# Latent attention of a two-block layer: tile-pipelined scores, rotary queries turned for two heads at once, the gated product in halves

## The reference

```python
q = (_rmsnorm(q_lat, q_lat_w) @ w_uq).reshape(B, L, 8, 128 + 64)
kv = (_rmsnorm(kv_lat, kv_lat_w) @ w_ukv).reshape(B, L, 8, 128 + 128)
q_nope, q_pe = q[..., :128], q[..., 128:]
k_nope, v = kv[..., :128], kv[..., 128:]
q_nope, k_nope = _rmsnorm(q_nope, qn_w), _rmsnorm(k_nope, kn_w)
q_pe = _rope(_rmsnorm(q_pe, qpe_w), cos, sin)
k_pe = _rope(_rmsnorm(k_pe, kpe_w), cos, sin)
s = q_nope @ k_nope.T + q_pe @ k_pe.T            # per head, 512 queries x 528 keys
p = softmax(s * 192 ** -0.5)
y_mla = (p @ v) * silu(g_mla)                    # g_mla: 1024 columns of the input projection
h_res = h_res + concat([y_mla, y_na]) @ w_out
```

## Time and profile before

| | |
|---|---|
| median of 3 runs (lowest to highest) | 1404.66 us (1404.48 to 1405.96) |
| profiled execution: its time, its span | 1407.8 us, 1406.1 us |
| PE busy, weight loads busy | 95%, 76% of the span |
| DVE, ACT, POOL busy | 51%, 36%, 43% |
| scores of head 0 to scores of head 7 (first tiles) | 792.56 to 984.33 us |
| last head and output projection, to the first product of the neighbourhood attention | 984.33 to 1055.88 us |

### The profile page before, as it was taken

The page is one execution under the profiler, slowest core; times in us unless marked ns, Lnnn a source line. Parts: engine busy times, 40 slices in busy tenths (PEclk is TensorE's granted clock), DMA queues, the critical chain, the costliest instruction groups (busy, mean ns, idle before and its releaser), DMA issues.

```text
span 1406.1 us, 20334 instructions
## 1 busy us (share of the span) xinstructions
PE 1335.3 (95%) x6958; PEld 1066.1 (76%) x6958; DVE 716.9 (51%) x1347; ACT 501.9 (36%) x1042; POOL 605.7 (43%) x366
## 2 busy tenths in 40 slices
PE   7999999998999999999985899999899999999997
PEld 6877777875888888888874677787778888888765
DVE  4237766644565565621142577777434544444441
ACT  3233333313333333310022566666202444444420
POOL 5423323363444445555530543544154655555511
PEclk9999999999999999999997999999989999999999
DMA  6322222232333333332331111111033322222112
GB/s 181 96 64 77 70 75 76 69 96 60 92 98 94 94 100 90 94 116 83 98 90 31 45 30 46 30 44 43 17 104 101 84 69 67 67 70 71 60 33 73
DMA packets 196561, 105.40 MB, mean 75 GB/s; under 512 B 18982, under 2 KB 194444, under 8 KB 196508
## 3 DMA queue, kind: packets, MB, share of 16 engines
q1 hardware_dynamic: 196060, 104.00, 26.0%
q0 software_dynamic: 432, 0.69, 0.2%
q10 hardware_dynamic: 16, 0.00, 0.0%
HBM read 102.57 MB, written 2.10 MB: 74 GB/s over the span
## 4 chain that ended last, share of the span: by engine, by line
PE 82%; issue 5%; DVE 4%; POOL 4%; ACT 3%; DMA 1%; SPq 0%; DVEq 0%; POOLq 0%; ACTq 0%
PE ps L348 20%; PE ps L349 19%; PE ps L350 19%; PE ps L370 9%; PE ps L1232 1%; PE ps L1262 1%; PE ps L1243 1%; POOL w_low L335 1%; PE ps L1265 1%; POOL y_low L656 1%; DMA x_tok<-in_x_dram 1%; PE ps L893 1%; PE ps L1286 1%; POOL sq L637 1%; PE ps L915 1%
## 5 line engine op out<-in xcount | busy, mean ns | idle before, releaser
L335 POOL TENSOR_TENSOR w_low<-w_raw,w_high 128x1024 fp32r<-128x1024 f32 x183 | 447.7, 2448 | 539.1 <-DVE w_high L330 539.0
L348 PE MATMUL ps<-h_high,w_high 128*128 128x512 f32 x864 | 353.5, 409 | 11.8 <-DVE h_low L471 8.4
L349 PE MATMUL ps<-h_low,w_high 128*128 128x512 f32 x864 | 343.8, 398 | 0.0
L350 PE MATMUL ps<-h_high,w_low 128*128 128x512 f32 x864 | 342.6, 397 | 0.0
L348 PEld LDWEIGHTS ps<-h_high,w_high 128*128 128x128 f32 x864 | 163.8, 190 | 62.3 <-issue 20.6
L330 DVE CAST w_high<-w_raw 128x1024 fp32r<-128x1024 f32 x183 | 137.3, 752 | 139.1 <-PE ps L350 75.1
L350 PEld LDWEIGHTS ps<-h_high,w_low 128*128 128x128 f32 x864 | 163.9, 190 | 37.7
L349 PEld LDWEIGHTS ps<-h_low,w_high 128*128 128x128 f32 x864 | 164.0, 190 | 35.2 <-issue 1.7
L2047 DVE SCALAR_TENSOR_TENSOR z<-ps,cv,z 128x511 f32<-128x511 f32 x44 | 33.0, 750 | 97.8 <-ACT z L1516 97.8
L1516 ACT ACTIVATE z<-ps,cv 128x512 f32<-128x512 f32 x44 | 34.3, 779 | 121.9 <-PE ps L350 121.7
L350 PE MATMUL ps<-m_high,w_low 128*128 128x512 f32 x176 | 69.4, 395 | 0.0
(11 more groups left out here) (327 smaller groups left out, 2405.7 us busy)
## 6 DMA issues: line engine op xcount, KB each, us to landing
w_raw<-in_w_in_dram SPq DMA_DIRECT2D x150, 256.0 KB, 3.2
w_raw<-in_w_up_dram SPq DMA_DIRECT2D x88, 256.0 KB, 3.1
w_raw<-in_w_out_dram SPq DMA_DIRECT2D x44, 256.0 KB, 3.0
w_raw<-in_w_down_dram SPq DMA_DIRECT2D x32, 256.0 KB, 3.0
w_raw<-in_w_down_dram SPq DMA_DIRECT2D x16, 192.0 KB, 2.7
rel<-in_rel_bias_dram SPq DMA_DIRECT2D x8, 384.0 KB, 3.2
x_tok<-in_x_dram SPq DMA_DIRECT2D x4, 512.0 KB, 5.8
w_raw<-in_w_ob_dram SPq DMA_DIRECT2D x8, 256.0 KB, 2.8
```

What stands on the lines that cost most here:

```text
L335: pool.tensor_tensor(w_low[:, n % RING, :], w_raw[:, n % RAW, :], w_high[:, n % RING, :].bitcast(F32), ALU.subtract).then_inc(low_made, 1)
L348: pe.matmul(acc, wh, mh, start=first and k == 0, stop=False)
L349: pe.matmul(acc, wh, ml, start=False, stop=False)
L350: done = pe.matmul(acc, wl, mh, start=False, stop=last and k == tiles - 1)
```

## The change

1. Rotary queries for two heads at once: the strip of an even head now has in its extra 64 columns the rotary columns of the next, odd head (`twice`), so that the 128 output rows hold both heads. `m_project(0)`, `m_sums(0)`, `m_rotate`, the square, the root and `m_rope` are then done for even heads alone. `q_pe` is a tile of its own. The low part of the rotary query is made per head on VectorE (`m_pe_low`), where GpSimd did it before.
2. `head` becomes `head_then_even` and `head_then_odd`, by the parity of the next head. In both, the scores of tile t + 1 stand ahead of the turning of tile t, and the turning of tile 3 moves into the next head. Scores wait for `s_exp`; the meta corner moves from bank 1 to the first 128 columns of bank 6, and so its transpose waits, in tiles 0 and 2, for the gated product (`s_y`) that reads them.
3. The scale is in the gains of the queries (`mq_gain`), the maximum is negated by the reduction, and ScalarE's small negating operation goes away. The main part of the probabilities is scaled ahead of the meta part.
4. The gate has two buffers (`mg`), and the gated product goes into a tile of its own (`gy`) in two halves.
5. `last_head`: more of the early output projection stands behind turnings, and strip `N_OM` + 3 is made early too. GpSimd makes strips `N_OM` + 6 and + 7 ahead of the bias table.

```diff
+                q_pe = sb("q_pe", [P, S], F32, a)[:]
+                a.enter_context(nc.sbuf_tensor("y_low_", [P, 7, S], F32))
+                gy = sb("gy", [P, S], F32, a)[:]
...
-                        ("twice", 704, 64, q[:, :, bass.ds(i * 96 + g * 192 + 128, 64)])]
+                        ("twice", 704, 64, q[:, :, bass.ds(i * 96 + g * 192 + (320 if g % 2 == 0 else 128), 64)])]
...
+            def m_pe_low(i, c):
+
+                dve.wait_ge(s["x_high"], i * 6 + (3 * c + 2))
+                own, other = (slice(h * 64, h * 64 + 64) for h in (c % 2, 1 - c % 2))
+                dve.tensor_tensor(qpe_parts[other, c % 2, :], q_pe[own, :], qpe_parts[own, c % 2, :].bitcast(F32),
+                                  ALU.subtract).then_inc(s["xp_low"], 1)
...
             pool.wait_ge(s["tables_in"], 64)
+            for n in range(N_OM + 6, N_OM + 8):
+                make_low(pool, n)
             bias_table(0, 0)
-            for n in range(N_OM + 6, N_NA + 5):
+            for n in range(N_OM + 8, N_NA + 5):
...
                 if not first:
-                    pe.wait_ge(s["s_meta"], i * 16 + (8 * c + 2 * t))
+                    pe.wait_ge(s["s_exp"], i * 8 + (4 * c + t))
...
-                pe.transpose(ps[0:80, 1, 3 * P:4 * P], me_meta[:, t % 2, :], ident[:])\
+                if t == 2 or c and t == 0:
+                    pe.wait_ge(s["s_y"], i * 4 + (2 * c + t // 2))
+                pe.wait_ge(s["s_probs"], i * 16 + (8 * c + 2 * t + 2))
+                pe.transpose(ps[0:80, 6, 0:P], me_meta[:, t % 2, :], ident[:])\
                     .then_inc(s["s_turned"], 1)
...
+            def head_then_even(i, c):
+
+                m_turn(i, c - 1, 3)
+                m_project(i, c + 1, 0)
+                m_project(i, c + 1, 1)
+                m_weigh(i, c - 1, 1)
+                m_sums(i, c + 1, 0)
+                m_scores(i, c, 1)
+                m_turn(i, c, 0)
+                m_gate(i, c + 1, 0)
+                m_sums(i, c + 1, 1)
+                m_rotate(i, c + 1)
+                m_scores(i, c, 2)
+                m_turn(i, c, 1)
+                m_project(i, c + 1, 3)
+                m_project(i, c + 1, 2)
+                m_weigh(i, c, 0)
+                m_sums(i, c + 1, 2)
+                m_scores(i, c, 3)
+                m_turn(i, c, 2)
+                m_gate(i, c + 1, 1)
+                m_turn_v(i, c + 1)
+                m_gate(i, c + 1, 2)
+                m_scores(i, c + 1, 0)
+
+            def head_then_odd(i, c):
+                if c:
+                    m_turn(i, c - 1, 3)
+                m_project(i, c + 1, 1)
+                m_project(i, c + 1, 3)
                 if c:
                     m_weigh(i, c - 1, 1)
-                m_project(i, c + 1, 0)
-                m_project(i, c + 1, 1)
+                m_scores(i, c, 1)
                 m_turn(i, c, 0)
-                m_sums(i, c + 1, 0)
-                m_scores(i, c, 1)
                 m_sums(i, c + 1, 1)
+                m_sums(i, c + 1, 2)
                 m_gate(i, c + 1, 0)
-                m_rotate(i, c + 1)
+                m_scores(i, c, 2)
                 m_turn(i, c, 1)
                 m_project(i, c + 1, 2)
-                m_scores(i, c, 2)
+                m_gate(i, c + 1, 1)
                 m_weigh(i, c, 0)
-                m_project(i, c + 1, 3)
-                m_gate(i, c + 1, 1)
+                m_scores(i, c, 3)
                 m_turn(i, c, 2)
-                m_sums(i, c + 1, 2)
-                m_scores(i, c, 3)
+                m_gate(i, c + 1, 2)
                 m_turn_v(i, c + 1)
-                m_gate(i, c + 1, 2)
-                m_turn(i, c, 3)
                 m_gate(i, c + 1, 3)
                 m_scores(i, c + 1, 0)
...
             def last_head(i, c):
+                m_turn(i, c - 1, 3)
+                pe.wait_ge(s["s_low"], 6)
+                pe.wait_ge(s["p_root"], 40)
+                early(0, (0, 6))
                 m_weigh(i, c - 1, 1)
-                pe.wait_ge(s["s_low"], 6)
-                pe.wait_ge(s["p_root"], 48)
-                early(0, (0, 6))
+                m_scores(i, c, 1)
                 m_turn(i, c, 0)
+                pe.wait_ge(s["mg_done"], 8)
+                early(1, (0, 5))
+                m_scores(i, c, 2)
+                m_turn(i, c, 1)
                 pe.wait_ge(s["s_low"], 7)
                 early(0, (6, 7))
-                m_scores(i, c, 1)
-                pe.wait_ge(s["mg_done"], 8)
-                early(1, (0, 5))
-                m_turn(i, c, 1)
                 early(1, (5, 7))
-                m_scores(i, c, 2)
                 m_weigh(i, c, 0)
                 pe.wait_ge(s["mv_low_"], 8)
-                early(2, (0, 3))
+                early(2, (0, 2))
+                m_scores(i, c, 3)
                 m_turn(i, c, 2)
-                early(2, (3, 5))
-                m_scores(i, c, 3)
-                early(2, (5, 7))
+                early(2, (2, 7))
                 m_turn(i, c, 3)
+                pe.wait_ge(s["s_copied_b"], 32)
+                early(3, (0, 1))
                 m_weigh(i, c, 1)
+                early(3, (1, 7))
...
-                early = m < EARLY
+                early = m < 4
...
                 act.wait_ge(s["s_top"], i * 8 + (4 * c + t + 1))
-                act.activation(mm_[:, t % 2, 1:2], mm_[:, t % 2, 0:1], ACT.Copy, scale=-MLA_SCALE)\
-                    .then_inc(s["s_neg"], 1)
-                act.wait_ge(s["s_neg"], i * 8 + (4 * c + t + 1))
-                act.activation(halves(me[:, t % 2, :]), wide(0), ACT.Exp, scale=MLA_SCALE,
-                               bias=mm_[:, t % 2, 1:2], accum_out=mm_[:, t % 2, 2:3]).then_inc(s["s_exp"], 1)
+                act.activation(halves(me[:, t % 2, :]), wide(0), ACT.Exp, bias=mm_[:, t % 2, 1:2],
+                               accum_out=mm_[:, t % 2, 2:3]).then_inc(s["s_exp"], 1)
...
-            def m_gated(i, c):
-                dve.wait_ge(s["s_summed"], i * 4 + (2 * c + 2))
+            def m_gated(i, c, p):
+                q = slice(p * 2 * P, (p + 1) * 2 * P)
+                dve.wait_ge(s["s_summed"], i * 4 + (2 * c + p + 1))
                 dve.wait_ge(s["mg_done"], i * 2 + (c + 1))
-                dve.tensor_tensor(gm[:], ps[:, 6, :], gm[:], ALU.mult).then_inc(s["s_y"], 1)
-
+                if c:
+                    dve.wait_ge(s["s_low"], i * 2 + c)
+                dve.tensor_tensor(gy[:, q], ps[:, 6, q], mg[:, c % 2, q], ALU.mult).then_inc(s["s_y"], 1)
...
+            def head_then_even(i, c):
+                ahead = N_MLA + 2 * (c + 1) + 3
+                m_top(i, c, 0)
+                m_rest(i, c - 1, 3)
+                m_scale(i, c, 0)
+                make_high(dve, ahead, i * 4)
+                m_gated(i, c - 1, 1)
+                m_gate(i, c)
+                m_top(i, c, 1)
+                m_normed(i, c + 1, 0)
+                m_rest(i, c, 0)
+                m_scale(i, c, 1)
+                m_rope(i, c + 1, 0)
+                m_normed(i, c + 1, 1)
+                m_top(i, c, 2)
+                m_rest(i, c, 1)
+                m_scale(i, c, 2)
+                m_rope(i, c + 1, 1)
+                m_keep(i, c + 1)
+                m_pe_low(i, c + 1)
+                m_gated(i, c, 0)
+                m_top(i, c, 3)
+                m_normed(i, c + 1, 2)
+                m_rest(i, c, 2)
+                m_scale(i, c, 3)
+                make_high(dve, ahead + 1, i * 4)
+                m_place_v(i, c + 1)
```

More of the change, by code:

```diff
@@ L421, in after, with heads, nth @@
                 eng.wait_ge(s[name], value)
+        def heads(c, even, odd):
+            return (even + odd) * (c // 2) + even * (c % 2)
+        def nth(c, item):
+            return item - c % 2
         def col(c):
@@ L1111, in m_rotate @@
             def m_rotate(i, c):
-                pe.wait_ge(s["p_normed"], i * 6 + (3 * c + 1))
-                pe.matmul(ps[:, 7, :], rot[:], q_f[:], start=True, stop=True).then_inc(s["qr_turned"], 1)
+                if c % 2:
+                    return
+                pe.wait_ge(s["p_normed"], i * 5 + (heads(c, 3, 2) + 1))
+                pe.matmul(ps[:, 7, :], rot[:], q_pe, start=True, stop=True).then_inc(s["qr_turned"], 1)
             def m_gate(i, c, part):
@@ L1656, in head @@
-            def head(i, c, more=True):
+                if c > 1:
+                    act.wait_ge(s["s_y"], i * 4 + (2 * c - 2))
+                g = mg[:, c % 2, :]
+                act.activation(g, ps[:, 5, :], ACT.Exp, scale=-1.0).then_inc(s["mg_part"], 1)
+                act.wait_ge(s["mg_part"], i * 6 + (3 * c + 1))
+                act.activation(g, g, ACT.Ln, bias=1.0).then_inc(s["mg_part"], 1)
+                act.wait_ge(s["mg_part"], i * 6 + (3 * c + 2))
+                act.activation(g, g, ACT.Exp, scale=-1.0).then_inc(s["mg_part"], 1)
@@ L1677, in head, with last_head @@
+                m_keep_v(i, c + 1)
+                m_expo(i, c, 3)
+                m_high_of(i, c + 1, 2)
                 m_copy(i, c, 2)
```

(20 more changed lines are left out.)

282 lines of the change are left out of this document (154 added, 128 removed).

## The result

The changed kernel takes 1385.55 us (median; 1383.43 to 1387.03), the kernel before beside it on the same chip 1404.95 (1404.48 to 1405.96). The ratio is 0.9853, with an interval of 0.9841 to 0.9865: 19.4 us faster, where 31.4 were forecast. The time lies inside the range that was given, 12 us above the predicted one, at rival A's 1385.

The account below looks back on a forecast made before the run. PE, busy 95% of the span, was taken as the bound. Gains of 20.6 (heads), 1.3 (prologue) and 9.5 (end), 31.4 us off the 1404.66 median, gave 1373.3 us; own range 1368 to 1380, with A and B 1364 to 1387.

Parts of the forecast that it names:

- rival A: VectorE late all over: every head waits as now, even ones 1.4 us more; 1385 us, chance 0.25.
- term 1: Heads: PE drops projection, sums and rotation in four odd heads, 3.31 us each; the stretch's work falls 13.6 us to 162.6.
- term 2: Waiting in the heads: 8.6 us against 15.6 now, even heads losing 1.8 each, odd 0.8; with term 1, 20.6 us gained.
- the prediction's own sign: Wrong if even heads take 28 us or more, the turning waits for `s_y`, or the heads' clock falls below 1.00.
- The rival theory of a VectorE too full: Rival in the experiment with GpSimd's order: VectorE's queue bounds even heads, PE's wait moves to the copy; under 0.5 us gained.
- term 3: Prologue: with `q_pe` apart the query copy starts about 1.2 us earlier; 1.3 us gained, from 0 to 1.5.
- costs nothing: `m_pe_low`, priced at 0.7 us on VectorE, stands where PE has other work; at worst 4.9 us.
- term 4: Last head and output projection: reordered work and fewer waits give 60.0 us, 11.5 less; 9.5 counted as gain.
- the 1.6 us given back: End: 1.6 us of the 11.5 gained, allowed for one stretch at the lower clock.
- B: Nearly all waits go: 0.4 us of waiting per head and no low clock; 1365.5 us, chance 0.14.
- D: Slower: waits in odd heads bring the clock to 1.2 GHz; with half the heads' work there, 1454 us; chance 0.03.
- C: Heads bound by a missed chain, shorter odd heads only wait more; nothing gained there or at the end; 1404 us, 0.03.

Follow-up runs that it names:

- the look-ahead undone: Kernel after with each turning put back ahead of the next tile's scores, pairing and halves kept: 1395.74 us, 0.9922.
- The experiment with GpSimd's order: Kernel after, but in even next heads GpSimd makes the strip's remainder between the two squares instead of behind them and `y_low`: 1379.56 us, 0.9806.
- the three edits: Kernel after with `m_keep` ahead of `m_rope`, GpSimd's remainder between the squares (both even next heads), and prologue copy and `m_pe_low` ahead of the rounding: 1370.91 us.
- the prologue's order: Kernel after with the prologue's query copy first, then `m_pe_low`, both ahead of the rounding that releases GpSimd's `w_low`: 1382.79 us, 0.9832.
- the reordered kernels: Kernels after with the prologue's copy and `m_pe_low` ahead of the rounding: alone 1382.79 us, with the three edits 1370.91, with the end filled besides 1370.38.
- the repeat: The kernel after, unchanged, measured once more as base for the experiments: 1384.47 us, 0.9849.
- before with GpSimd's new order: Kernel before with only GpSimd's remainders of strips 6 and 7 moved ahead of the bias table: 1398.97 us, 0.9954.
- with the end filled besides: The three edits plus two early tiles of strip 3 ahead of the last weighing, without the copy wait, and three kept for behind `y_low`: 1370.38 us.

## Why the prediction was right or wrong

**Right: what bounds, and the price of PE's work.** One matmul by the distance of starts gave the odd heads (22.68 for 22 to 23), and, once the two long holds were out of the way, the even ones (25.46 for 25.4). The 1.36 us for a doubled projection confirms term 1 by itself. It holds only with the look-ahead: without it the odd heads were 2.8 us longer. The heads' gain of 14.9 us is thus the 13.6 of term 1 and little more. Against 162.6 us of work there were 14.3 us of waiting left, with 15.6 before and 8.6 forecast, and 25.9 with the look-ahead undone.

**Failed: term 2, the even heads and the first head.** The heads lost 5.7 us against the forecast. The even ones took 28.42 for 27.2, three times 1.2. By the prediction's own sign (28 us or more) its picture of them was wrong, though the total stayed inside the range. The step that failed is "two-input operations, which take 0.77 us alone and 1.56 beside GpSimd's 2.38 us `w_low`": they stand still until GpSimd is done. In the new order VectorE comes to the normalizing just as GpSimd goes from `y_low` into `w_low`, so it costs 2.94 us, and the rotation waits 0.8 us where I had written "none". The copy's wait was near (1.6 for 1.4), but the 0.83 us of the cosine product that I put into it was itself the price of a hold; it is 1.61 here. The experiment with GpSimd's order shows the cause: same work, a hold of 0.3 us instead of 2.4, 1.8 us back per even head. I had put what lateness there was at the copy. The rival theory of a VectorE too full is out: with the three edits its work is the same and no even head waits, with VectorE busy for 21.6 of 25.46 us.
The first head took 23.6 us, where the same sum gave 20.9 (22.1 and 0.8, less 1.54 and 0.46). I had counted it as an odd head less a weighing and a turning, but the work missing there was the cover for its own chain: 1.6 us of waiting for `mp_low`, 1.1 for `mv_meta`. The second goes with the prologue's order; the first stays in the kernel with all three edits.

**Failed: term 3, the prologue.** For 1.3 less came 1.95 more. The step is `m_pe_low` "costs nothing", and with it "the copy can start about 1.2 us earlier". In the prologue it stands right behind the rounding that starts GpSimd's `w_low` and ahead of the copy; held for 2.87 us it makes PE wait 3.5, and then comes a stretch at the lower clock level, 1.2 GHz (granted clock 0.50 from 785.90 to 791.50):

```profile
785.90 2.04 PE L1121 MATMUL ps<-sq,ones 128*128 128x512 f32 x2 [3.49 <-DVE q_f L2227]
...
788.17 0.63 PE L354 MATMUL ps<-h_low,w_high 128*128 128x512 f32 x1
788.59 0.63 PE L355 MATMUL ps<-h_high,w_low 128*128 128x512 f32 x1
```

Nine matmuls took 4.6 us, with the other order 2.5. The wait for `qn_low` of the earlier trace rows went in exchange, and comes back as 2.6 us in the reordered kernels.

That is a second miss in this term: the 1.3 us aren't there without the hold either. With the other order the copy does start 1.1 us earlier (15.1 us into the prologue, 16.2 before), but the prologue takes 22.05 to 22.45 us in the three kernels that have it, and 22.39 and 22.29 in the two traces with the code of before. The chain behind the copy loses what was won: the normalizing of `q_f` is held by the `w_low` that now runs from 784.83 to 787.22, so PE still waits for `qn_low`:

```profile
785.97 1.79 DVE L2235 SCALAR_TENSOR_TENSOR q_f<-q_f,mq_gain,root 128x512 f32<-128x512 f32 x1 [1.23 <-ACT root L1659]
```

Inside the loop, at 887.82 above, `m_pe_low` does cost 0.69 and nothing on the path.

**Right but for one wait: term 4, the end.** 61.5 us for 60 to 62, and nearly each step in its place: no wait for the last `y_low`, 1.7 for a `w_low` at strip 4 (1.9 forecast), strips 6 and 7 free of the table. The clock is 1.00, so the 1.6 us given back for it weren't due. Instead there is a wait of 0.7 at strip 6, where none was forecast, because GpSimd waits for the table's DMA ahead of the two remainders; that the two errors have opposite signs is luck:

```profile
1007.20 0.50 PE L353 MATMUL ps<-y_high,w_high 128*128 128x512 f32 x1 [1.73 <-POOL w_low L340]
...
1019.32 0.50 PE L353 MATMUL ps<-y_high,w_high 128*128 128x512 f32 x1 [0.68 <-POOL w_low L340]
```

**What is left.** The stages together gave 14.9 - 1.95 + 10.0 = 23.0 us for 31.4, 8.4 of the 12 us. The medians show 19.4 and 21.4 us (the latter in the repeat). The other 3.6 us belong to no stage: the medians differ by less than the two profiled executions do (24.4 us). The profiled execution of before is 2.9 us above its median and that of after 2.1 below; in the former the latent attention began at 770.17, in the latter at 767.85. Over all traces it began between 767.4 and 770.3, and with the very same code ahead at 770.17 and 767.47 (before, and before with GpSimd's new order) or at 767.67 and 770.31 (with the three edits, and with the end filled besides): one profiled execution carries 2 to 3 us that the change has no part in. What makes that start vary stays open, and so does what the small parts of the change (the negation, the two gate buffers, the halves) are worth by themselves.

Of the rivals, A had the time right, but by luck and with another reason. Its heads gain 8.9 us, where 14.9 came; the prologue and the spread between executions brought the sum back to its figure. Not every head waited as before (the odd ones have none listed). The even ones and the prologue did, by the hold; the first head waited for want of cover. B, nearly no waiting, is out for this kernel: an even head waits 1.6 and 0.8 us. D is out: the heads' clock is 1.00 in the kernel after, with waits up to 1.6 us, and also in the one with the look-ahead undone, with 11.5 us more:

```profile
792.74:981.27 188.53, 170.02 (x1072) 144.39 (x1070) 136.75 (x279) 109.25 (x228) 72.81 (x44) 1.00 0.14 39
```

C fell with the odd heads.

## What to carry to other kernels

Price a VectorE operation with two SBUF inputs by when it comes, not by an average from its neighbourhood: here it ended 0.55 us after the GpSimd operation that it met, and after the next one too where it came in the last 0.07 us of the first. When a change moves such an operation, lay GpSimd's queue of the new order beside it; often it is enough to start the long GpSimd operation while VectorE waits for something else, and to put a copy that TensorE waits for ahead of the operation that will be held. Work taken from the bounding engine counts in full only while enough of it is left over each chain of the other engines, and the first pass of a pipeline has less of it than the others.

## What the runs showed of the hardware that was not expected

- A held VectorE operation ends 0.54 to 0.56 us after the GpSimd operation that held it, in 34 of 34 cases, while alone it takes 0.68 to 0.77: some 0.15 to 0.2 us of its own time lie under the hold.
- GpSimd can keep VectorE out over two of its operations in a row: `y_low`, then `w_low`, 2.94 us in all for VectorE. It did so in the three places where VectorE came in the last 0.05 or 0.06 us of the first, and in none of the four where VectorE had waited 0.3 us or more.
- It goes the other way too. A `w_low` that starts while VectorE is in such an operation takes longer (start, us):

```profile
906.39 0.76 DVE L2235 SCALAR_TENSOR_TENSOR scaled<-scaled,cv,root 128x528 f32<-128x528 f32 x1
...
906.55 2.84 POOL L340 TENSOR_TENSOR w_low<-w_raw,w_high 128x1024 fp32r<-128x1024 f32 x1 [2.06 <-DVE w_high L335]
```

2.84 us for 2.37: 0.47 more, of the 0.60 us that were left of VectorE's operation.
